# The third modulation summed in the second mixer, and the first dense layer in two phases by seven products

## What is computed

```python
cs = jax.nn.silu(c)
for i in range(DEPTH_2):                                  # 2 layers
    mod = cs @ ada_w[i] + ada_b[i]                        # 1024 x 6144
    sh1, sc1, g1, sh2, sc2, g2 = jnp.split(mod, 6)
    h = rms_norm(x, norm_mix_g[i]) * (1 + sc1) + sh1
    mix = hybrid_mixer_2(h, ...) if i % 2 == 0 else conformer_conv(h, ...)
    x = x + g1 * mix
    h = rms_norm(x, norm_ffn_g[i]) * (1 + sc2) + sh2
    x = x + g2 * ((jax.nn.silu(h @ wg[i]) * (h @ wu[i])) @ wd[i])
return rms_norm(x, final_norm_g)
```

## Time and profile before

| what | us |
|---|---|
| median of 3 runs (lowest to highest) | 1462.46 (1460.65 to 1464.28) |
| the profiled execution | 1465.13 |
| its span, first to last instruction | 1463.4 |
| PE busy | 1376.3 (94%) |
| DVE busy | 870.7 (60%) |
| ACT busy | 275.6 (19%) |
| POOL busy | 265.6 (18%) |
| moved from and to HBM | 355.58 MB, 243 GB/s |

### The profile page before, as it was taken

One profiled execution on the slowest core, in us unless ns is written; L12 is line 12 of the kernel. 1 busy time (PEld: TensorE's weight loads), 2 busy tenths in 40 slices (PEclk: granted clock), 3 DMA queues, 4 the chain that ended last, 5 costly groups with the idle time before them and its releaser, 6 DMA issues. The chain is left out here.

```text
span 1463.4 us, 18944 instructions
## 1 busy us (share of the span) xinstructions
PE 1376.3 (94%) x7517; PEld 1015.5 (69%) x7517; DVE 870.7 (60%) x1464; ACT 275.6 (19%) x602; POOL 265.6 (18%) x342
## 2 busy tenths in 40 slices
PE   5999999896776999999999999999999999999997
PEld 1877655653442788768888888777766878888843
DVE  2458775432232668753454685788783874777864
ACT  2222221000000311643345101000002113211101
POOL 5078010000000300553355402100020100000000
PEclk9999999998888999999999999999999999999999
DMA  9976887899999697866774455898854552555431
GB/s 350 310 263 226 285 329 298 348 417 415 416 418 385 191 305 261 306 194 162 159 180 133 160 162 176 327 333 322 297 210 150 155 156 73 163 168 172 170 129 47
DMA packets 176057, 355.58 MB, mean 243 GB/s; under 512 B 7289, under 2 KB 137041, under 8 KB 158561
## 3 DMA queue, kind: packets, MB, share of 16 engines
q1 hardware_dynamic: 166720, 313.64, 60.4%
q0 software_dynamic: 9248, 40.71, 9.5%
HBM read 352.58 MB, written 1.74 MB: 242 GB/s over the span
## 5 line engine op out<-in xcount | busy, mean ns | idle before, releaser
L1846 PE MATMUL PS<-HT,ring 128*128 128x256 f32 x1152 | 258.3, 382 | 0.1
L1846 PEld LDWEIGHTS PS<-HT,ring 128*128 128x128 f32 x1152 | 215.5, 190 | 36.0 <-issue 7.9
L1542 DVE TENSOR_TENSOR X<-X,PS 128x1024 f32<-128x1024 f32 x14 | 17.1, 1222 | 113.2 <-PE PS L1318 113.2
L1265 PE MATMUL PS<-ring_extra,slot_rows 128*32 128x256 f32 x576 | 56.3, 450 | 27.6 <-DMA ring_extra<-in_expert_w_gate 7.1
L2876 PE MATMUL PS<-HT,ring 128*128 128x256 f32 x352 | 76.8, 379 | 0.0
L2905 PE MATMUL PS<-ada_stage,half_sums 128*128 128x256 f32 x320 | 75.6, 379 | 0.0
L2905 PE MATMUL PS<-ring,half_sums 128*128 128x256 f32 x320 | 75.6, 379 | 0.0
L2876 PEld LDWEIGHTS PS<-HT,ring 128*128 128x128 f32 x352 | 66.7, 190 | 9.0
L2882 PE MATMUL PS<-ring,hid 128*128 128x512 f32 x160 | 71.8, 592 | 0.0
L2905 PE MATMUL PS<-ring,HT 128*128 128x256 f32 x304 | 68.8, 379 | 0.0
L2905 PEld LDWEIGHTS PS<-ring,half_sums 128*128 128x128 f32 x320 | 59.4, 190 | 11.2 <-issue 4.3
(11 more groups left out here) (736 smaller groups left out, 2465.4 us busy)
## 6 DMA issues: line engine op xcount, KB each, us to landing
ring<-in_hy_w_in SPq DMA_DIRECT2D x40, 1024.0 KB, 8.4
ring_extra<-in_w_ada SPq DMA_DIRECT2D x24, 1024.0 KB, 7.9
ada_stage<-in_ada_w POOLq DMA_DIRECT2D x24, 1024.0 KB, 7.3
ring<-in_ffn_w_gate SPq DMA_DIRECT2D x22, 1024.0 KB, 5.9
ring<-in_ffn_w_up SPq DMA_DIRECT2D x22, 1024.0 KB, 5.8
ring<-in_ffn_w_down SPq DMA_DIRECT2D x22, 1024.0 KB, 5.8
ring_extra<-in_expert_w_down SPq DMA_DIRECT2D x18, 1024.0 KB, 22.9
ring_extra<-in_expert_w_up SPq DMA_DIRECT2D x18, 1024.0 KB, 20.1
```

The lines of the kernel that those rows point to most:

```text
L1265: mm = pe.matmul(PS[e * SLOTS:(e + 1) * SLOTS, 2, j * CW:(j + 1) * CW], hs[:, k, e * SLOTS:(e + 1) * SLOTS], w[e][:, k, :], start=(k == 0) ...
L1542: dve.tensor_tensor(part, part, PS[:, 6:8, :], ALU.add).then_inc(added, 1)
L1846: mm = pe.matmul(dst, w[:, k, half * P:(half + 1) * P], HT[:, k, :], start=(k == 0), stop=(k == KT - 1))
```

## The change

1. The 24 adds of the third modulation go from the first dense layer into the second mixer, to the quarters `THIRD_ADDS` in steps 14 to 35. SP fetches their pieces (1 MB, in one buffer at first, from the seventh piece on in two). Sums, rows and columns for both halves are made there (`sum_third`, `turn_third`, `finish_third`). PE's `value` waits for the first columns from m = 3 on, `out_half(0, 1)` for the second.
2. The 16 adds of the second modulation come earlier (steps 1 to 13), from two buffers.
3. The convolution's first tap goes from DVE to ACT (`tap`).
4. The first dense layer takes the code of the second, in two phases by seven products. Its first sums of weights are made on DVE between `combine_a(1)` and `combine_b(1)`.
5. Small loads: `small_loads` has 13 instead of 16, seven more follow in `later_loads`. In the tail there are 11 instead of 13. GpSimd has no modulation to fetch, and builds `tap_blocks` behind the first dense layer, since the layer uses that memory.

```diff
-    segment("ffn0", [ffn_source(0)(k, e) for k, e in expert_order(FFN_CHUNKS)])
+    SPLIT_ORDER = [(k, e) for e in range(FFN_CHUNKS) for k in "gu"] + [("d", e) for e in range(FFN_CHUNKS)]
+    segment("ffn0", [ffn_source(0)(k, e) for k, e in SPLIT_ORDER])
...
+        third_stage = [ap.rearrange("p (a n) -> p a n", a=2) for ap in (stage[:], BC[:].rearrange("p a s -> p (a s)"))]
+        second_stage = (third_stage[0], third_acc[:, 0:5:4, :])
...
-        add_at = {(s, 3): s - 2 for s in range(2, 18)}
+        SECOND_ADDS = [(1, 3), (2, 3), (3, 0), (3, 3), (4, 0), (4, 3), (5, 3), (6, 3), (7, 0)] + [(s, 3) for s in range(7, 14)]
+        THIRD_ADDS = ((14, 1), (15, 2), (16, 3), (18, 0), (19, 1), (20, 1), (21, 1), (21, 3), (22, 1), (22, 3), (23, 1), (23, 3),
+                      (25, 0), (25, 3), (26, 2), (28, 0), (29, 3), (31, 0), (31, 2), (32, 1), (32, 3), (34, 1), (34, 3), (35, 2))
...
+        third_rows_at = {(29, 1): 0, (36, 1): 1}
+        third_copy_at = {(29, 2): 0, (36, 2): 1}
+        third_turn_at = {(29, 3): 0, (36, 3): 1}
+        third_finish_at = {(30, 0): 0, (37, 1): 1}
...
+                def fetch_third(n):
+                    if n == 0:
+                        sp.wait_ge(summed, ADDS - 1)
+                    elif n == 6:
+                        sp.wait_ge(used, base + V0 + 3)
+                    else:
+                        sp.wait_ge(third_summed, third_before(n) + 1)
+                    sp.dma_start(third_stage[third_buffer(n)], wv3[:, n % KT, THIRD_PIECES[n // KT], :])\
+                        .then_inc(third_in[third_buffer(n)], 16)
...
+                    if m >= 3:
+                        pe.wait_ge(third_made, 1)
...
+                def sum_third(c):
+                    pe.wait_ge(third_summed, THIRD_READY[c])
+                    pe.wait_ge(moved_att, THIRD_MOVED[c])
+                    for g in range(4):
+                        v = third_acc[:, 1 + g // 2, :].rearrange("p (m h k) -> p h k m", h=2, k=KT // 2)[:, g % 2]
+                        mm = pe.matmul(PS[32 * g:32 * g + 32, 7, :], ones[:, 0:32], v, start=True, stop=True,
+                                       tile_position=(0, 32 * g))
+                    mm.then_inc(third_rowsum, 1)
+                def turn_third(c):
+                    pe.wait_ge(third_rowcopy, c + 1)
+                    for k in range(KT // 2):
+                        mm = pe.transpose(PS[:, 7, k * P:(k + 1) * P], third_rows[:, k * P:(k + 1) * P], ident[:])
...
+                    for m in range(2):
+                        tile = 2 * XORDER[s] + m
+                        act.activation(conv_tiles(s)[:, m, :], RX[:, s % 3, m, 0:S], ACT.Identity, ...
+                def add_third(n):
+                    g, k, b = n // KT, n % KT, third_buffer(n)
...
+                    if k == 0:
+                        dve.tensor_scalar(THIRD_HOMES[g], third_stage[b], cv[:, 0:1], None, ALU.mult).then_inc(third_summed, 1)
+                    else:
+                        dve.wait_ge(third_summed, n)
+                        dve.scalar_tensor_tensor(out=THIRD_HOMES[g], in0=third_stage[b], scalar=cv[:, k:k + 1],
+                                                 in1=THIRD_HOMES[g], op0=ALU.mult, op1=ALU.add).then_inc(third_summed, 1)
...
                 combine_a(1)
+                first_gate, first_up = (segs["ffn0"].base + j for j in range(2))
+                for n in (first_gate, first_up):
+                    dve.wait_ge(landed[slots[n]], 16 * turns[n])
+                step(dve.tensor_tensor(t1, up[:, 0:4, :], gate[:, 0:4, :], ALU.subtract))
+                step(dve.tensor_tensor(t2, up[:, 4:8, :], t1, ALU.subtract))
+                step(dve.tensor_tensor(up[:, 0:4, :], up[:, 4:8, :], up[:, 0:4, :], ALU.subtract))
+                step(dve.tensor_tensor(t4, gate[:, 4:8, :], t2, ALU.subtract))
                 combine_b(1)
...
             turn(0)
-            ffn(0, 0, turn_vectors, modulation_rows)
-            modulation_columns()
-            gate_rows(1, 0, 0)
-            pe.wait_ge(gated, 4)
-            turn(1)
+            for e in range(FFN_CHUNKS):
+                split_gate_up(0, e, 0)
+                if e == 0:
+                    turn_vectors()
+            for gi in range(len(DOWN_GROUPS)):
+                split_down(0, gi)
+            whole_down(0)
+            turn_row(1, 0)
+            gate_rows(GATE_MIX, 0)
+            turn_row(1, 1)
...
-            pool.wait_ge(left, 4)
-            pool.memset(acc[:], 0.0).then_inc(zeroed, 1)
...
+            pool.wait_ge(small, SMALLS)
+            pool.wait_ge(left, 2 * 4)
             for at, m in enumerate(PE_TILES):
```

More of the change, by code:

```diff
@@ L1688, in small_loads, with later_loads @@
                     (rowc[:, 2, :], t["hy_d_skip"][0].partition_broadcast(P)),
+                    (quarter_sum[:], t["const_one_block"]),
                     (cv[:], t["c_2"][0].rearrange("(p k) -> p k", k=KT)),
+                ]
+                for dst, src in loads:
+                    pool.dma_start(dst, src).then_inc(small, 16)
+        def later_loads(pool):
+            pool.wait_ge(small, SMALLS)
+            with nc.allow_non_contiguous_dma(reason="small vectors"):
+                loads = [
                     (gain_ffn[:], t["norm_ffn_g"][0].rearrange("(p k) -> p k", k=KT)),
@@ L2877, in half_rows @@
                 return mm
-            def down_part(n, par, f, first=False):
-                w = w_slot(n, D)
-                for i, h in pieces():
-                    mm = pe.matmul(PS[:, 4 + 2 * i + h, :], hid[:, par, f, i * P:(i + 1) * P],
-                                   w[:, f, h * 512:(h + 1) * 512], start=first and f == 0, stop=False)
-                return mm
-            def last_down(f, n, par):
-                w = w_slot(n, D)
-                for i, h in pieces():
-                    for a in range(2):
-                        mm = pe.matmul(PS[:, 4 + 2 * i + h, :], hid[:, par, a, i * P:(i + 1) * P],
-                                       w[:, a, h * 512:(h + 1) * 512], start=False, stop=(a == 1))
-                    if (i, h) != (TT - 1, 1):
-                        mm.then_inc(downed, 1)
-                mm.then_inc(used, 1)
             def turn_vectors():
@@ L2929, in seven @@
                 hs7 = lambda j: [hsum[:, j, k, :] for k in range(4)]
-                ws7 = lambda j: [wsum[:, e % 2, j, k, :] for k in range(4)]
-                arrive(pe, n_g)
-                arrive(pe, n_u)
-                pe.wait_ge(combined, weights_summed(f, e))
-                if e > 1:
-                    pe.wait_ge(combined, row_sum(f, e - 1, 2))
-                product(P2, rows(1, 0), half(gate, 1))
-                product(P1, rows(0, 0), half(gate, 0)).then_inc(used, 1)
-                if e > 1:
-                    pe.wait_ge(combined, row_sum(f, e - 1, 5))
@@ L3248, in _ @@
             root(0, 0)
             turn(0, mod[:, 3, :], mod[:, 2, :])
-            act.wait_ge(small, SMALLS)
-            act.activation(cv[:], cv[:], ACT.Silu).then_inc(silu_c, 1)
-            ffn(0)
+            act.activation(idle[:, 0:1], ident[:, 0:1], ACT.Silu)
+            gate_and_move(0)
             act.activation(idle[:, 0:1], ident[:, 0:1], ACT.Sqrt)
-            squares_of_pieces(1, pieces(), x_done, 0, 8)
-            act.wait_ge(moved, M_COLUMNS)
+            squares_of_pieces(1, LAST_PIECES, x_done, 0, 8)
@@ L3724, in _program @@
     tail.close()
+    carry.close()
 def _constants(np):
```

696 lines of the change are left out of this document (259 added, 437 removed).

## The result

After the change the kernel takes 1472.32 us (median of six runs, 1468.31 to 1474.20) against 1462.56 before. The ratio taken over all runs is 1.0061, 95% interval 1.0046 to 1.0076. It is slower by 9.8 us; I had forecast 1459.8 and a range up to 1467.0.

What follows compares the result with a forecast made beforehand. PE's instructions set the time nearly everywhere; work moved on DVE is free while DVE keeps its dates with PE. The terms sum to -2.7 us, taking the median from 1462.46 to 1459.8 us; range 1453.5 to 1467.

Steps and rivals of the forecast that it cites:

- first dense layer: First dense layer takes the second's code and should reach about its time: 207.5 for 220.7 us, 13.2 less.
- transition to the convolution mixer: From the last down matmul's end to the convolution mixer's first projection: 6.7 for 5.2 us, 1.5 lost.
- PE's sums and turns in the mixer: Second mixer: two sums of rows at 1.95 us and 8 turns at 0.9 on PE, 4.8 us lost whole.
- gaps in the v steps: PE's two gaps of 0.63 us behind DVE in the v steps should go: 1.3 us gained (bounds 0 and 1.3).
- adds 6 to 11: Steps 21 to 23: adds in half steps make the first bias 3 to 5 us later; price 0 to 5, taken 1.5.
- attention steps: Attention steps: `sum_third(0)` waits 0.7 us for ACT, the columns for `value(3)` as much: 1.5 us (bounds 0.7 and 5).
- step 34: Adds 21 and 22 stand ahead of slot 15's scaling on DVE; PE stands still 1.9 to 3.3 us, taken 2.5.
- The second, DMA binding: Attention steps: DMA share 0.98; pieces landing over 9.7 us behind request delay DVE, then PE: 1468.7 us; chance 0.13.
- Rival 3: First dense layer doesn't reach its template, small loads and a waiting gate copy lose 4 us: 1463.8 us; chance 0.06.
- Rival 4: Attention slots: DVE adds and POOL additions exclude each other, making scaled rows later: +4, 1464 us; chance 0.06.
- Nothing for either: Small loads in two groups and later `tap_blocks` cost nothing; POOL's queue has no date near.
- Profile and median: Whole kernel: the profiled execution, forecast at 1462.4 us, stands 2.7 us above the median, forecast at 1459.8.

Runs made afterwards that it cites:

- experiment 2: The kernel after with add 21 at (33, 2) and add 22 at (35, 0), behind slot 15's scaling instead of ahead of it: 1468.4 us.
- experiment 9: The kernel after with only one of each bias table's three groups fetched (128 KB for 384 KB), pieces whole: 1460.0 us.
- experiment 4: The kernel after with the second pair of bias tables asked for at (23, 1), not with the first pair at (22, 2): 1468.9 us.
- Experiment 5: The kernel after with filler matmuls (80 in the trace, 17.4 us) on PE just ahead of its wait in `turn(0)`: 1478.4 us.
- experiment 8: The even kernel: the kernel after with the 24 third adds spread evenly, two gate adds last, first row sum after 14 adds: 1456.1 us, ratio to before 0.9964.
- experiment 11: The kernel of experiment 8 with all twenty small loads of the mixer in one group, none waiting for another: 1467.5 us.
- experiment 1: The kernel after with third adds 10 to 14 placed later, from (23, 3) to (26, 3): 1467.9 us.
- 3: The kernel after with the moves of experiment 1 and experiment 2 together: 1465.7 us.
- experiment 10: The kernel of experiment 8 with the second pair of bias tables at (23, 1) and the first sum of rows at (29, 2): 1461.5 us.
- 12: The kernel of experiment 8 with only the second pair of bias tables moved to (23, 1): 1459.8 us, ratio to before 0.9974.
- experiment 6: The kernel after with only the first 128 of 1024 columns of each third modulation piece fetched, all adds and waits kept: 1465.4 us.

## Why the prediction was wrong

From the mixer's start on, in the profiled executions:

| term of the sum | forecast | measured |
|---|---|---|
| first dense layer | -13.2 | -12.95 (207.73 for 220.68) |
| transition to the convolution mixer | +1.5 | +1.2 (6.40 for 5.20) |
| PE's sums and turns in the mixer | +4.8 | +4.8 |
| gaps in the v steps | -1.3 | -1.4 (190.30 for 191.71) |
| adds 6 to 11 | +1.5 | +12.1 (9.1 idle, 3.0 slow) |
| attention steps | +1.5 | +0.6 (`sum_third(0)`'s wait) |
| step 34 | +2.5 | +4.6 (2.8 idle, 1.7 slow) |
| not forecast: convolution mixer | 0 | +0.9 |
| sum | -2.7 | +9.8 (the spans say +10.1) |

**Right.** The layer, and its count of matmuls; the transition (its terms add up to 6.5 us, not to the 6.7 that I wrote), whose lines are

```profile
1122.60 7.03 PE L3069 MATMUL PS<-ring,hid_slab 128*128 128x512 f32 x16
1132.19 1.16 PE L2942 MATMUL PS<-ident,xn 128*128 128x128 f32 x8 [2.56 <-DVE xn L3281]
...
1136.03 3.69 PE L2959 MATMUL PS<-HT,ring 128*128 128x256 f32 x16
```

(the layer ends at 1129.63, the projection starts 6.40 behind it); PE's new work, 1.95 twice and 0.9 for the turns; the v steps; `sum_third(0)` waiting for ACT, 0.56 for my 0.7; and the order on DVE at step 34, 2.83 for my 1.9 to 3.3, which experiment 2 took away.

**The step that failed** is the one on adds 6 to 11: "Price 0 to 5; I take 1.5, nearer to the lower end, since the idle time absorbs most." It priced the bias tables only, 3 to 5 us later, and there it was right (3.0). It never asked when the piece of add 10 lands, which stands ahead of slot 1's biasing and slot 0's scaling on DVE: 21.6 us behind its request, and PE lost 12.1 us by it. A better reckoning sets everything asked for against the engines' rate. Between 660.09 and 668.86 SP asks for three pieces and two ring chunks, 5.24 MB, POOL for 1.57 MB of tables. At the rates above that is 14.6 + 8.2 = 22.8 us from about 661, to 684; the add began at 684.58. That is rough: the two requests made last, behind piece 10's, landed at 687.0 and 689.8, and the rates come from the same 23 us, so the agreement is no test. The rates of the kernel before are one. These are its queues from 655 to 692 us:

```profile
q1 hardware_dynamic: 4160, 4.19, 38.7%
q0 software_dynamic: 448, 1.57, 20.0%
```

4.19 MB in 14.3 us and 1.57 MB in 7.4 give 17.9 + 7.4 = 25 us and a landing at 686. I had written in words that the bias transfers mostly occupy the engines by being slow and had counted them as harmless for it; they cost nearly twice their bytes, 8.2 us of the 22.8, and without two thirds of them the gap was gone (experiment 9).

**The second fault** is in both large terms: I priced PE's waits at their length. Each was followed by a stretch at a lower clock that cost a third to two thirds as much again, 4.7 us in all. It isn't a fixed price: in experiment 4 the same gap before `turn(15)`, 2.82 us, was followed by a clock of 1.00 and cost nothing more (4.04 us from 801.39 to 805.43, for 3.99). Nothing in the profile before shows that inside the mixer, since its only gaps there, 0.63 us each, leave the clock at 1.00. The expert stage ahead of it has such stretches, and I hadn't read it. Experiment 5 shows the link.

**The rivals.** The second, DMA binding, had the right mechanism: a piece landing over 9.7 us behind its request. Its size, 13.4 us, is near by luck, since it was made of four late pieces and two late bias slots, and the trace has one late piece and a slow clock. I gave it 0.13 because I tested it on the mean: a share of 0.98 over the attention steps. As engine time that was right (0.98 of 123.7 us is 121, 0.83 of 143.85 is 119), yet the even kernel runs without the gaps at 0.87. The mean did not decide; the five requests within 9 us beside the tables did, in a place that I had priced as another term. Rival 3 (the layer) is out: it reached its template. Rival 4 has its mechanism in the trace, but not its price. An add on DVE and an addition on POOL exclude each other, and the rule that the prediction takes from the Trainium skill (SBUF — State Buffer, Who interferes with whom) agrees: POOL's, 0.73 us when alone, takes 2.85 beside an add that starts 0.08 us earlier:

```profile
691.39 2.34 DVE L2506 SCALAR_TENSOR_TENSOR third_acc<-ada_stage,ada_c,third_acc 128x2048 f32<-128x2048 f32 x1
691.47 2.85 POOL L2774 TENSOR_TENSOR rows_q<-rows_q,x_scores 128x256 f32<-128x256 f32 x1
695.09 0.73 POOL L2774 TENSOR_TENSOR rows_q<-rows_q,x_scores 128x256 f32<-128x256 f32 x1
```

Where POOL was first, the add took up to 2.81 in these steps. Between the two gaps no such place passes a wait on to PE. At step 34 it may have a part: POOL ends the last row of slot 15 at 805.07, behind the second add (804.49), and the runs do not separate the two.

**Right for a wrong reason: the small loads.** "Nothing for either" holds for the change as made. But the second group is no bookkeeping. With all twenty loads, four of them new, in the group that PE waits for, 10 us are gone at the mixer's start (experiment 11). I had said that POOL's queue has no date near; it has one.

**Profile and median.** I took the median to lie 2.7 us below the profiled execution. It lay 4.0 above: the profiled execution was the fastest of the six. That it had one of the shortest starts (478.95) fits, but the others have no profile.

**Open.** The convolution mixer is 0.9 to 1.7 us longer in every kernel with the change, 116.1 to 116.9 for 115.2. Most of it is one pause of 0.8 to 1.6 us in PE's issue that nothing in the profile explains and that the kernel before doesn't have. And single executions differ by 16 us in experiment 1 and by 12 to 13 in 3 and 4, but by 6 in the kernel after, whose adds stand as close, and by 6 to 7 in the even ones with two groups of small loads (8, 10, 12). Late pieces may make the spread; each kernel has one profile, so it isn't shown.

## What to carry to other kernels

When an edit adds transfers with dates, don't price them by the landing time of one and don't ask whether the mean share stays under 1: list what is asked for in the stretch ahead of each date, divide each kind by its own rate from the trace (MB over share times time), and compare the sum with the date. Put the work that waits for a transfer behind, not ahead of, the work that the busiest engine waits for, and spread the requests; the same 24 MB cost 12 to 16 us less when they came evenly (experiments 12 and 8), 4.6 of them by the new order at step 34. And price a wait of the matmul engine above its length as soon as it is some microseconds long: here 9.09 us cost 12.1, 5.39 cost 10.15, and 2.8 cost 2.8 to 4.6.

## What the runs showed of the hardware

- The granted clock was 0.50 for 5.5 us behind 9.09 us without work, 0.71 in the 5.8 us behind 2.83, 0.63 in the 4 us behind 2.97 (experiment 4), and 1.00 behind the gaps of 0.63. Behind 2.44 us (experiment 6) and 2.69 (experiment 1) the same 24 matmuls took their 5.45 as ever.
- The same gap did not always do the same: behind 2.82 us before `turn(15)` the clock stayed at 1.00 in experiment 4, and behind 2.56 us ahead of the convolution mixer it fell to 0.69 in experiment 10 and stayed at 1.00 in the kernel after and in experiment 8.
- An addition on POOL beside an add on DVE took 2.85 us for 0.73.
- 1.57 MB of bias tables took as much of the DMA engines' time as 3.0 MB of weights, 0.19 against 0.36 MB a us.
- A transfer of 128 KB took 14.9 us to land behind a burst, and 3.0 in the median.
- Seven small loads more in the group that PE waits for made it wait 5.4 us and cost 10 us.
